# A hybrid attention and state-space decoder step: the sample convolution moved into the in-projection, decays clamped on GpSimd, the causal mask added by TensorE

## What is computed

```python
def _latent_attention(q_lat, q_rope, ckv, k_rope, q_pos, k_pos):
    sc = (einsum('bqhr,bkr->bhqk', q_lat, ckv) + einsum('bqhe,bke->bhqk', q_rope, k_rope)) * SOFTMAX_SCALE
    sc = where(k_pos <= q_pos, sc, NEG_BIG)          # causal mask
    p = softmax(sc)

def _causal_conv(xbc, prev, lw):                     # width 4, over x, B and C
    xp = concatenate([prev, xbc], axis=1)
    acc = conv_b + sum(xp[:, k:k + s, :] * w[k] for k in range(4))
    return silu(acc)

def _ssd_chunked(xs, dt, da, bm, cm):                # chunks of 128 tokens
    decay_in = exp(_segsum(a))                       # exp(acum[l] - acum[s]) for s <= l, else 0
    cb = einsum('bclgn,bcsgn->bcgls', cc, bc)        # C times B, one for each group and chunk
    y_diag = einsum('bcgls,bgjcls,bcsgjp->bclgjp', cb, decay_in, xdt)
```

## Time and profile before

| | |
|---|---|
| median of three runs | 618.04 us (617.41 to 618.86) |
| the profiled execution | 621.36 us |
| its span | 619.3 us |
| mean granted TensorE clock | 0.952 |
| busy: TensorE matmul, VectorE, ScalarE, GpSimd | 546.9, 393.7, 281.3, 111.4 us |

### The profile page before, as it was taken

How to read it: one execution, slowest core, us unless ns; L and a number is a source line. 1 busy time by engine, 2 the same in 40 slices (tenths; PEclk the granted TensorE clock), 3 DMA queues, 4 the chain that set the end, 5 groups by cost and what they waited for, 6 DMA issues and landing times.

```text
span 619.3 us, 12350 instructions
## 1 busy us (share of the span) xinstructions
PE 546.9 (88%) x4716; PEld 461.1 (74%) x4716; DVE 393.7 (64%) x756; ACT 281.3 (45%) x607; POOL 111.4 (18%) x126
## 2 busy tenths in 40 slices
PE   4999989999999999999986899896896568888993
PEld 4999989999888888888873365564543368878992
DVE  5575986815666677434432565757486989996574
ACT  7233221124665554552513544564676646734430
POOL 3110000000000000000003533486253501110520
PEclk9999999969999999999998799989798779999998
DMA  8242123364888888888744210541460065569562
GB/s 339 80 143 87 53 77 104 108 224 155 260 286 263 265 260 269 260 258 281 234 142 131 60 53 11 105 99 42 147 254 3 14 270 189 188 206 355 205 171 70
DMA packets 55691, 104.11 MB, mean 168 GB/s; under 512 B 7193, under 2 KB 25986, under 8 KB 55378
## 3 DMA queue, kind: packets, MB, share of 16 engines
q1 hardware_dynamic: 55634, 103.33, 51.5%
HBM read 95.68 MB, written 7.73 MB: 167 GB/s over the span
## 4 chain that ended last, share of the span: by engine, by line
PE 60%; DVE 20%; ACT 6%; issue 5%; DMA 5%; POOL 2%; SPq 2%; DVEq 0%; ACTq 0%; POOLq 0%
PE pm L1456 14%; PE pm L1458 12%; PE pm L1457 12%; PE px L1539 4%; DVE w_lo L847 4%; PE px L1555 3%; DMA w_raw<-in_w_out 3%; DVE hring L1138 2%; PE pm L1674 2%; PE px L1721 1%; PE pm L1712 1%; DMA stS<-in_conv_state 1%; SPq L390 1%; DVE prod L1145 1%; PE px L1722 1%
## 5 line engine op out<-in xcount | busy, mean ns | idle before, releaser
L1456 PE MATMUL pm<-xw_hi,w_lo 128*128 128x260 f32 x544 | 163.7, 301 | 9.3 <-DVE w_lo L961 8.2
L1457 PE MATMUL pm<-xw_lo,w_hi 128*128 128x260 f32 x544 | 155.7, 286 | 0.0
L1458 PE MATMUL pm<-xw_hi,w_hi 128*128 128x260 f32 x544 | 155.4, 286 | 0.0
L1456 PEld LDWEIGHTS pm<-xw_hi,w_lo 128*128 128x128 f32 x544 | 104.4, 192 | 24.5 <-issue 11.9
L530 ACT ACTIVATE w_hi<-w_raw 128x1024 fp32r<-128x1024 f32 (+1 forms) x70 | 72.1, 1036 | 104.1 <-PE pm L1458 82.4
L1457 PEld LDWEIGHTS pm<-xw_lo,w_hi 128*128 128x128 f32 x544 | 104.6, 192 | 0.2
L1458 PEld LDWEIGHTS pm<-xw_hi,w_hi 128*128 128x128 f32 x544 | 104.5, 192 | 0.0
L847 DVE TENSOR_TENSOR w_lo<-w_raw,w_hi 128x1024 fp32r<-128x1024 f32 (+1 forms) x70 | 85.6, 1228 | 28.4 <-ACT w_hi L530 28.3
L1456 PE MATMUL pm<-mix_hi,w_lo 128*128 128x260 f32 x256 | 74.4, 291 | 14.2 <-DVE w_lo L847 7.6
L1458 PE MATMUL pm<-mix_hi,w_hi 128*128 128x260 f32 x256 | 73.0, 285 | 0.0
L1456 PEld LDWEIGHTS pm<-mix_hi,w_lo 128*128 128x128 f32 x256 | 49.0, 191 | 16.6 <-DVE w_lo L847 9.7
(11 more groups left out here) (264 smaller groups left out, 1119.2 us busy)
## 6 DMA issues: line engine op xcount, KB each, us to landing
page<-in_cache SPq DMA_DIRECT2D x128, 288.0 KB, 3.5
w_raw<-in_w_in SPq DMA_DIRECT2D x34, 512.0 KB, 5.1
w_raw<-in_w_out SPq DMA_DIRECT2D x32, 512.0 KB, 6.2
dec<-ac_dram SPq DMA_DIRECT2D x16, 256.0 KB, 10.3
hring<-in_ssm_state SPq DMA_DIRECT2D x8, 512.0 KB, 8.8
o_ssms<-hring SPq DMA_DIRECT2D x8, 512.0 KB, 6.5
w_raw<-in_w_qb SPq DMA_DIRECT2D x6, 384.0 KB, 2.9
xraw<-in_xT SPq DMA_DIRECT2D x4, 520.0 KB, 6.3
```

Source lines behind the costliest of these rows:

```text
L1456: pe.matmul(out, wl, xh, start=start, stop=False)
L1457: pe.matmul(out, wh, xl, start=False, stop=False)
L1458: return pe.matmul(out, wh, xh, start=False, stop=stop)
```

## The change

1. `sample_conv` runs on VectorE after `lo(36)`, at item 34 of the in-projection; SyncE issues its load at item 31, after a wait for the twelfth `silu_x`, into the space of `u0`; ScalarE takes its two SiLUs at item 36.
2. GpSimd's `masked` no longer adds a mask of -1e30 in one instruction over four chunks: in four instructions, one for each chunk, it subtracts the row's own sum and clamps at zero. ScalarE takes one exponential of 128x512 without bias for each head.
3. VectorE multiplies C times B by the 0/1 triangle from PSUM, once for each group, ahead of `scaled_x(0)`; ScalarE's two copies go.
4. TensorE adds the causal mask in PSUM, by a matmul of a rounded identity and a rounded mask inside each block of scores; VectorE's addition goes. ScalarE rounds the two 128x128 constants at item 11.

```diff
@@ SyncE, loop over the items
+            if i == 31:
+                sp.wait_ge(a_silu, XT)
+                sp.dma_start(stS, a["conv_state"]).then_inc(s_sts, 16)
             for n in steps(i + 1):
                 load_pages(n)
...
-        sp.wait_ge(p_pv, 2)
-        sp.dma_start(stS, a["conv_state"]).then_inc(s_sts, 16)
@@ ScalarE
+            if i == 11:
+                act.wait_ge(s_const, 16)
+                act.activation(mask_r, cm[:, M_MQ, :], ACT.Copy).then_inc(a_mask, 1)
+                act.wait_ge(a_mask, 1)
+                act.activation(ident_r, cm[:, M_ID, :], ACT.Copy).then_inc(a_mask, 1)
...
+                if i == ZT[11] + 1:
+                    act.wait_ge(v_cs, 1)
+                    act.wait_ge(g_last, XT)
+                    act.activation(xbc[:, 0:8, NT:TT], cvs[:, 0, 0:8], ACT.Silu).then_inc(a_cvs, 1)
+                    act.activation(cvs[:, 1], cvs[:, 0], ACT.Silu).then_inc(a_cvs, 1)
...
-            for c in range(NCH):
-                act.activation(dec[:, h % 6, CH * c:CH * c + CH], dec[:, h % 6, CH * c:CH * c + CH], ACT.Exp,
-                               bias=nacum[:, SH * c + h:SH * c + h + 1]).then_inc(a_dec, 1)
+            act.activation(dec[:, h % 6, :], dec[:, h % 6, :], ACT.Exp).then_inc(a_dec, 1)
...
-        for g in range(2):
-            act.wait_ge(p_cb, g + 1)
-            act.activation(cbt[:, g, :], px[:, 2 + g, :], ACT.Copy).then_inc(a_cp, 1)
         for t in range(12, 16):
             silu_z(t)
-        act.wait_ge(v_cs, 1)
-        act.activation(xbc[:, 0:8, NT:TT], cvs[:, 0, 0:8], ACT.Silu).then_inc(a_cvs, 1)
-        act.activation(cvs[:, 1], cvs[:, 0], ACT.Silu).then_inc(a_cvs, 1)
@@ VectorE
+        def sample_conv():
+            dve.wait_ge(s_sts, 16)
+            dve.wait_ge(a_rt, 6)
+            link(dve.tensor_tensor(cvs[:, 0], xbc[:, :, NT:TT], taps[:, :, 3:4].to_broadcast(new), ALU.mult))
+            for k in range(3):
+                link(dve.tensor_tensor(cvs[:, 1], stS[:, :, k, :], taps[:, :, k:k + 1].to_broadcast(new), ALU.mult))
+                link(dve.tensor_tensor(cvs[:, 0], cvs[:, 0], cvs[:, 1], ALU.add))
+            dve.tensor_tensor(cvs[:, 0], cvs[:, 0], cols[:, C_CB:C_CB + XT].unsqueeze(2).to_broadcast(new), ALU.add)\
+               .then_inc(v_cs, 1)
...
+            if i == ZT[11] - 1:
+                sample_conv()
...
-            dve.wait_ge(a_dec, NCH * (h + 1))
-            dve.wait_ge(a_cp, 4)
+            dve.wait_ge(a_dec, h + 1)
...
-            link(dve.tensor_tensor(x[:, P * b:P * b + P], x[:, P * b:P * b + P], cm[:, M_MQ, :], ALU.add))
...
+        def masked_cb(g):
+            dve.wait_ge(p_cb, g + 1)
+            dve.tensor_tensor(cbt[:, g, :].rearrange("p (c l) -> p c l", c=NCH),
+                              px[:, 2 + g, :].rearrange("p (c l) -> p c l", c=NCH),
+                              cm[:, M_TRI:M_TRI + 1, :].to_broadcast([P, NCH, CH]), ALU.mult).then_inc(v_cb, 1)
+        masked_cb(0)
+        masked_cb(1)
+        dve.wait_ge(v_cb, 2)
         for n in range(2 * NCH):
             scaled_x(n)
-            if n == 2:
-                sample_conv()
@@ GpSimd
-            x = dec[:, h % 6, :].rearrange("p (c l) -> p c l", c=NCH)
-            pool.tensor_tensor(x, x, cm[:, M_ML:M_ML + 1, :].to_broadcast([P, NCH, CH]), ALU.add).then_inc(g_acm, 1)
+            for c in range(NCH):
+                x = dec[:, h % 6, CH * c:CH * c + CH]
+                last = pool.tensor_scalar(x, x, nacum[:, SH * c + h:SH * c + h + 1], 0.0, ALU.add, ALU.min)
+            last.then_inc(g_acm, 1)
@@ TensorE
+            if h == 0:
+                pe.wait_ge(a_mask, 2)
             for b in range(4):
...
                 pe.matmul(px[:, n % 3, 0:w], q[:, h, P * b:P * b + P], kn[:, h % 2, 0:w], start=True, stop=False)
+                pe.matmul(px[:, n % 3, P * b:w], ident_r, mask_r, start=False, stop=False)
```

More of the change, by code:

```diff
@@ L171, in build @@
     btok = at("btok", [P, NCH, GR, NS], F, G_ + 20480)
-    stS = at("stS", [P, XT, 3, NB], F, H_ + 5 * TB)
-    cvs = at("cvs", [P, 2, XT, NB], F, H_ + 5 * TB + 1152)
+    stS = at("stS", [P, XT, 3, NB], F, H_ + TB)
+    cvs = at("cvs", [P, 2, XT, NB], F, H_ + 5 * TB + 1024)
     kn = at("kn", [P, 2, NT], F, G_ + 10240)
@@ L199, in build @@
         small[name] = at(name, shape, F, o)
+        if name == "cm":
+            CM_ = o
         if name == "qlp":
@@ L219, in build @@
     nmh, alpha, rs, lsum, epsc, nmx, rsum = (small[k] for k in ("nmh", "alpha", "rs", "lsum", "epsc", "nmx", "rsum"))
+    ident_r = at("ident_r", [P, P], R, CM_ + 4 * P * M_MQ)
+    mask_r = at("mask_r", [P, P], R, CM_ + 4 * P * M_ML)
     def col(c):
@@ L246, in build @@
     s_hl, s_hst = [sem(f"state_loaded{s}") for s in range(NB)], sem("state_stored")
+    v_cb = sem("cb_masked")
+    a_mask = sem("mask_rounded")
     s_ukl = [sem(f"w_uk_loaded{s}") for s in range(2)]
@@ L947, in sample_out_t @@
             dve.tensor_copy(olT[:, :, g, :], px[:, 2, KVR:2 * KVR].rearrange("p (r n) -> p r n", r=2)).then_inc(v_ol, 1)
+        taps = cols[:, C_CW:C_CW + 4 * XT].rearrange("p (t k) -> p t k", k=4)
+        new = [P, XT, NB]
+        def sample_conv():
[7 more added lines that the diff above has]
+               .then_inc(v_cs, 1)
         dve.wait_ge(s_cols, 16)
@@ L1748, in _ @@
         pe.wait_ge(a_cvs, 2)
-        pe.wait_ge(a_cp, 4)
+        pe.wait_ge(v_cb, 2)
         pe.transpose(px[0:32, 3, 0:P], cvs[:, 1, 8:12, :], cm[:, M_ID, :]).then_inc(p_bct, 1)
```

## The result

The changed kernel takes 616.6 us in the median of 15 runs (613.54 to 618.39). The kernel before takes 621.05 in 15 runs (617.41 to 623.97), the first three of which are those ahead of the prediction. The ratio is 0.9935 (95% interval 0.9915 to 0.9956): faster by about 4.4 us (0.65%), where 18 were forecast. The profiled run took 617.29, with a span of 615.5 and a mean granted clock of 0.957.

A forecast was written before the change was run, and what follows sets the result against it. It took TensorE to bound the projections and, between them, a stall and chains through several engines. Its terms, 10.9 - 0.5 + 7.65 = 18.05 us off the median 618.04, gave 600.0 us; range 594 to 608.5.

The forecast's parts named there:

- The stall: Between the projections: TensorE's hole before 343.57 us (8.93) and the slow round behind it (2.26) would go, 11.2 us.
- The in-projection: The sample convolution's work, moved there, would be mostly covered: 0.5 us lost, between 0 and 1.5.
- The mask matmul: Attention heads: each of TensorE's 32 matmuls of 128 columns would take 0.15 us, between 0.06 and 0.22.
- the price of the GpSimd piece: Decay step: 0.376 us for each 128x128 piece, four making 1.50 a head against 1.41 for one addition.
- part 1: Between the projections: 11.2 us from moving the sample convolution, less 0.3 for the masked C times B, 10.9 gained.
- part 3: The attention loops: 7.05 + 1.2 - 0.6 = 7.65 us gained, with 0.6 lost in heads 0 and 1.
- The prediction's own sign of being wrong: Loops' ends still 17 us apart, or TensorE waiting for anything else between 328 and 352 us.
- rival C: GpSimd pieces cost more than assumed: loss 72p - 36.2 at price p, gain gone at 0.75; chance 0.03.
- ring: Loops s = 1, 2, 3: a chain through VectorE, ScalarE and TensorE sets their length; 2.35 us less a loop.
- A: Attention loops keep their period because GpSimd or TensorE's matmuls come last: 604 to 609 us, chance 0.15.
- B: Between the projections, late decay loads replace the stall: 1 to 3 us, 602 us; chance 0.10.
- D: Better than forecast: the low clock around 480 to 510 us recovers partly, 5 us, 592 to 596; chance 0.09.

The follow-up runs named there:

- old decay step: The changed kernel with its decay step undone (one GpSimd mask addition, four exponentials a head): 608.41 us, ratio 0.9793; measured again 606.47 us, ratio 0.9758.
- first probe: The changed kernel with four different pairs of operations in a head's four GpSimd pieces, decays not the right ones: 611.9 us in one run.
- cheap pieces: The changed kernel with (mult, add) in place of (add, min) in all GpSimd pieces, decays not the right ones: 602.57 us, ratio 0.9708.
- second price probe: The changed kernel with GpSimd's decay step at whole width for even heads, four other operations for odd ones, decays not right: 604.97 us in one run.

## Why the prediction was wrong

**The stall, right.** The sum had 11.2 us for the hole and the slow round behind it. The convolution alone shortens the stretch by 34.6 - 23.4 = 11.2. With the masked C times B beside it (0.3 lost in the sum) it is 34.6 - 23.7 = 10.9, as summed, once the pieces are cheap. One part of the working was too simple: it counted 2.26 us for a low clock that would not come back. In most of the shortened kernels the granted clock falls later instead (0.50 and 0.70 between 360 and 368, above). That loss does not stand in the stretch of the sum but in the first heads, below.

**The in-projection, not contradicted.** values_up(0) starts at 328.59 after and 328.37 before, 0.2 lost where the sum has 0.5. That is too small to be read from two profiles: the kernel with the old decay step starts it at 328.22 in one profile and at 326.04 in the other. The eight convolution steps lie between 280.47 and 282.8 in the trace of after, and TensorE's busy tenths in the page's slices there are nines, as in the earlier trace rows.

**The mask matmul, right.** 0.11 measured, 0.15 taken.

**The term that failed: the price of the GpSimd piece.** The sum read it from a row of another operation, L1371 (mult, add) at 0.376; measured were 0.72 undisturbed and 0.776 in the mean. In the sum this price is the "nothing" of part 1, where GpSimd was given 2.9 us against a round of 3.02, and the 0.1 more for each head in part 3. What came in its place is 5.8 us in the rounds, 5.7 in the loops and 1.3 between them. The prediction's own sign of being wrong came too: TensorE waits at 346 to 348 us, inside its 328 to 352. The row it was read from has the engine, the shape and the form of the operands, but not the operation.

The text named the price as rival C, gave it 0.03, and named reasons for it that are not the main ones: data that VectorE's neighbours contend for, and a second step. The first probe shows that a second step makes no such price when it is arithmetic (0.37) and that min costs 0.35 more; what may be contention is the 0.06 between the median of 0.72 and the mean. C's formula, 72p - 36.2 (its own terms give 36.3), has 19.7 us of loss at the measured mean of 0.776 and so 619.7; measured were 616.6. It is 3 us too dear, because it charges each of the three loops with 16 pieces, while there are ten heads and so 40 pieces: GpSimd's timeline has 8 of them in s = 1 and 16 in each of the other two (where the first starts 0.6 us early). With two loops charged instead of three it gives 9.0 + 7.0 us, 616.0. That this is so near is partly chance, for the places do not fit as well: in the loops the traces have 5.7, and in the rounds, where the formula has 6 x (1.42 + 4 x 0.776 - 3.02) = 9.0 us, they have 29.5 - 23.7 = 5.8. The first steps had GpSimd's 2 us in hand, and TensorE's waits begin only in the last three rounds. The Trainium skill, GPSIMD Engine Reference, "3.1 Elementwise — side-by-side cycle accounting", which the prediction weighed, charges each instruction two dispatch hops; the probe agrees that splitting costs (0.32 us for a further piece), but the compare weighs more.

**The loops, right in sum and wrong in place.** The sum had 2.35 us for each of the loops s = 1, 2, 3. The distances from the first score of one head to that of the next are:

| | before | after | cheap pieces | sum, for cheap pieces |
|---|---|---|---|---|
| heads 0 and 1 | 18.6 | 18.9 | 21.8 | 19.2 |
| s = 1 | 16.9 | 15.5 | 15.1 | 14.55 |
| s = 2 | 17.7 | 22.0 | 17.7 | 15.35 |
| s = 3 | 22.4 | 20.5 | 17.1 | 20.05 |
| s = 4 | 11.3 | 10.6 | 10.6 | 10.6 |
| s = 5 | 11.3 | 11.5 | 11.5 | 11.15 |
| rest, to the output projection | 32.9 | 32.4 | 31.9 | 32.55 |

With cheap pieces the three loops gain 1.8 + 0 + 5.3 = 7.1 us, where 7.05 were forecast. That the sum fits is luck: one loop gave nothing and another twice its share, and two profiles of one kernel differ by 1.6 us in s = 3 alone (21.0 and 19.4 with the old decay step). The ring was taken from one head for all three loops, and that head lies in s = 2 (405.38 to 423.10), the loop that gave nothing. The trace shows what the ring left out there. In the kernel with cheap pieces GpSimd has no gap at the start of the loop, which begins at 397.01:

```profile
396.40 3.23 POOL L1372 TENSOR_SCALAR dec<-dec,nacum 128x128 f32<-128x128 f32 x8
399.60 1.26 POOL L1411 TENSOR_TENSOR gacc<-sq,sq 128x512 f32<-128x512 f32 x1
400.84 3.54 POOL L1372 TENSOR_SCALAR dec<-dec,nacum 128x128 f32<-128x128 f32 x8
404.36 0.82 POOL L1393 TENSOR_SCALAR pr<-pr,rsum 128x128 f32<-128x128 f32 x2
```

ScalarE waits 2.40 and 1.19 us for the first eight of these pieces, VectorE 0.45 and 0.93 for ScalarE, and the first y_pair starts 6.9 us into the loop, where before it was 6.5. The ring of the earlier trace rows does get shorter, in the second half of the loop, and the first half and a slightly lower clock (0.98) take that back. This is read from one profile; no experiment tested it. Heads 0 and 1 lose 3.2 instead of 0.6, at the low clock; the second price probe, which keeps its clock, has 18.9 there. As made, the change loses 4.3 us in s = 2, where GpSimd is busy 17.51 of 18, and the gains elsewhere only cancel that.

**The rivals.** A was right that another member of the ring comes last and that it is GpSimd, but it put this down to GpSimd's room and not to a price; at the row's price the whole gain is there (cheap pieces, 0.9708), though in s = 2 GpSimd's pieces still come late, as shown above. B: GpSimd waits for the decay loads 5.5 us over the span, has 6.9 for them before; no new wait. D: no gain beyond the sum.

**Does it add up?** By ratio the convolution alone gives -1.45%, the TensorE mask alone -0.37%, the decay step alone +0.71%: together -1.1%, measured -0.65%. The decay step costs 4 us on the kernel before but 8 to 11 on top of the rest. A part of GpSimd's longer queue lay in the hole, and that is gone: in the kernel with the decay step alone, GpSimd still idles 6.25 and 1.91 us ahead of xdte at 344.09 and 350.17, where the changed kernel has no gap. That it is this and nothing else was not tested.

## What to carry to other kernels

A price may be taken from a neighbouring row only if that row has the same operation, not the same engine and shape alone; arithmetic and compare are different operations, and where no row has the operation, the upper bound has to carry its share of the chance. Put the price at which the gain is gone beside the likeliest one: here the factor was two, and two unlike operations on the same engine and shape turned out to differ by just that. And an edit that moves work to an engine with room (12 of 18 us) should be counted again with the hole that it had until then taken out.

## What was new about the hardware

- On GpSimd, a tensor_scalar of 128x128 in f32 takes 0.37 us with add and multiplication, 0.53 with min alone, 0.72 with min or max and one more step; over 128x512, min and add take 1.92, while a tensor_tensor addition takes 1.27.
- On VectorE the same add and min take 0.22 us a piece, against 0.72 on GpSimd (a piece without min was not measured on VectorE). Beside GpSimd's 128x512 tensor_tensor of 1.27 us two of four pieces lasted 1.3 us each, and the four 2.94 instead of 0.87.
- A low granted clock (0.50) that stood behind a hole of 9 us came up again at 360 us once the hole was gone, in a stretch where TensorE is busy without a gap; it did not in the second price probe, with the same matmuls within a microsecond of that time. Runs of one kernel then differ by their mean granted clock: 602.99 us at 0.970 and 611.46 at 0.956.
